# A third input piece queued at once instead of after the second, and 32 more dummy matmuls at the start, in a hybrid decoder block

## The reference

```python
u = rms_norm(h, norm_mix)
q, k, v, z, g_att, g_pool = split(u @ w_in)       # q, k, v: 3 groups x 8 heads x 64
q, k = partial_rope(q, pos), partial_rope(k, pos) # first 16 of 64 dims
att = dilated_attention(q, k, v)                  # (window, dilation): (128,1), (512,4), (2048,16)
pooled = (multiscale_pool(z) @ w_pool_group) * pool_scale
merged = sigmoid(g_att) * (att @ w_att_branch) + sigmoid(g_pool) * (pooled @ w_pool_branch)
h = h + merged @ w_out
f = rms_norm(h, norm_ffn)
h = h + (silu(f @ w_gate) * (f @ w_up)) @ w_down  # D_FF = 2816
return rms_norm(h, norm_final)
```

## Time and profile before

| | |
|---|---|
| median of 3 runs | 1144.56 us (1142.74 to 1144.61) |
| profiled execution | 1144.56 us; its slowest core is core 1 (odd) with a span of 1143.0 us |
| spans of the odd cores 1, 3, 5, 7 | 1143.0, 1134.1, 1136.5, 1134.3 us |
| spans of the even cores 0, 2, 4, 6 | 1128.6, 1130.4, 1128.0, 1132.3 us |
| TensorE busy on core 1 | 1112.9 us, 97% of the span |
| VectorE, ScalarE busy on core 1 | 532.0 us (47%), 448.9 us (39%) |

### The profile page before, as it was taken

How to read it: one execution, slowest core, us unless ns; L and a number is a source line. 1 busy time by engine, 2 the same in 40 slices (tenths; PEclk the granted TensorE clock), 3 DMA queues, 4 the chain that set the end, 5 groups by cost and what they waited for, 6 DMA issues and landing times.

```text
span 1143.0 us, 21157 instructions; the slowest of 8 cores (1128.0 to 1143.0 us)
## 1 busy us (share of the span) xinstructions
PE 1112.9 (97%) x8267; PEld 650.0 (57%) x8267; DVE 532.0 (47%) x795; ACT 448.9 (39%) x725; POOL 69.5 (6%) x135
## 2 busy tenths in 40 slices
PE   5999998999999999999999999999999999999996
PEld 4767766657685867544444444444444444444476
DVE  2478454754763736856543484121223342333244
ACT  2585464675675655562222132111121133231121
POOL 3111000000000000001200000000000000000000
PEclk9899999999999999999999999999999999999999
DMA  8967235227224334152480416443345344641512
GB/s 189 322 178 190 59 79 117 49 62 144 42 58 80 72 80 128 31 142 36 67 198 1 83 30 132 81 74 74 74 75 93 59 88 104 141 91 66 102 72 72
DMA packets 39959, 109.49 MB, mean 96 GB/s; under 512 B 4720, under 2 KB 10992, under 8 KB 36016
## 3 DMA queue, kind: packets, MB, share of 16 engines
q0 software_dynamic: 18800, 68.43, 31.5%
q1 hardware_dynamic: 19760, 38.14, 11.2%
q10 hardware_dynamic: 1296, 1.51, 0.5%
HBM read 145.80 MB, written 15.73 MB: 141 GB/s over the span
## 4 chain that ended last, share of the span: by engine, by line
PE 91%; DMA 4%; DVE 3%; ACT 1%; issue 1%; SPq 0%; DVEq 0%; ACTq 0%
PE ps_all L458 90%; DMA arena<-xs 2%; DVE arena L476 1%; DVE arena L481 1%; ACT arena L466 1%; DMA arena<-sb_1 1%; DMA sa_1<-arena 0%; DMA sb_1<-arena 0%; SPq L323 0%; DVE arena L485 0%; PE ps_all L695 0%; SPq L355 0%; DVE arena L517 0%; DVEq L341 0%; DVEq L348 0%
## 5 line engine op out<-in xcount | busy, mean ns | idle before, releaser
L458 PE MATMUL ps_all<-arena 128*128 128x128 bf16 (+5 forms) x8220 | 1111.6, 299 | 22.3 <-ACT arena L466 9.7
L458 PEld LDWEIGHTS ps_all<-arena 128*128 128x128 bf16 (+1 forms) x8220 | 646.8, 104 | 484.5 <-issue 34.4
L466 ACT ACTIVATE arena<-ps_all 128x512 bf16<-128x512 f32 (+10 forms) x505 | 310.9, 642 | 484.3 <-PE ps_all L458 477.5
L476 DVE TENSOR_TENSOR arena<-arena 128x1024 bf16<-128x1024 bf16 (+14 forms) x314 | 230.7, 754 | 149.0 <-ACT arena L466 117.4
L476 DVE TENSOR_TENSOR arena<-ps_all,arena 128x496 bf16<-128x496 f32 (+4 forms) x160 | 115.3, 730 | 300.7 <-PE ps_all L458 294.1
L466 ACT ACTIVATE arena<-arena 128x512 f32<-128x512 f32 (+8 forms) x187 | 114.9, 632 | 134.6 <-DVE arena L476 99.7
L481 DVE SCALAR_TENSOR_TENSOR arena<-arena 128x512 bf16<-128x512 f32 (+6 forms) x172 | 99.5, 632 | 50.7 <-ACT arena L466 49.5
L481 DVE SCALAR_TENSOR_TENSOR arena<-arena,ps_all 128x496 f32<-128x496 f32 (+1 forms) x64 | 42.0, 665 | 63.5 <-PE ps_all L458 63.2
L323 POOL DMA_DIRECT2D arena<-wq x36 | 19.2, 541 | 247.4 <-PE ps_all L458 245.1
L466 ACT ACT_TABLE_LOAD x13 | 16.7, 1283 | 43.2 <-PE ps_all L458 39.3
L323 POOL DMA_DIRECT2D arena<-wgu x22 | 11.6, 529 | 300.6 <-PE ps_all L458 242.5
(11 more groups left out here) (10 smaller groups left out, 10.8 us busy)
## 6 DMA issues: line engine op xcount, KB each, us to landing
arena<-wgu POOLq DMA_DIRECT2D x22, 1024.0 KB, 8.8
arena<-xT POOLq DMA_DIRECT2D x24, 512.0 KB, 16.2
arena<-wd POOLq DMA_DIRECT2D x8, 1408.0 KB, 10.4
arena<-wq POOLq DMA_DIRECT2D x36, 256.0 KB, 5.6
arena<-wb POOLq DMA_DIRECT2D x24, 256.0 KB, 5.5
arena<-xT SPq DMA_DIRECT2D x8, 768.0 KB, 10.2
oT<-arena SPq DMA_DIRECT2D x24, 248.0 KB, 2.1
arena<-xs POOLq DMA_DIRECT2D x4, 512.0 KB, 24.5
```

Source lines behind the costliest of these rows:

```text
L458: return P.op("pe", lambda e: e.matmul(out, lhsT=lhsT, rhs=rhs, start=start, stop=stop, **kw), [lhsT, rhs], [out], (busy, 0.17))
L466: return P.op("act", lambda e: e.activation(out=out, in_=in_, func=func, **kw), rd, [out], (width(in_) / 1200 + 0.11 + load, 0.08))
L476: return P.op("dve", lambda e: e.tensor_tensor(out=out, in0=in0, in1=in1, op=op), [in0, in1], [out], cost_dve(out, in0, in1))
```

## The change

Two edits. `WARM` of Second goes from 76 to 108. And SyncE no longer waits for the second piece before it issues the third; the line that told the planner that SyncE is busy until 6.0 goes with it. `load_piece` returns nothing any more, which has no effect.

```diff
-WARM = (64, 76)
+WARM = (64, 108)
...
         for lo in range(8 * a, 8 * b, 1024):
-            tok = P.dma(q, f32(K.XS[k][0] + lo, 1024), T["xs"][k][:, lo:lo + 1024])
-        return tok
+            P.dma(q, f32(K.XS[k][0] + lo, 1024), T["xs"][k][:, lo:lo + 1024])
...
     P.dma("sp", cstv, T["cst"])
     load_piece(0, 0, "act")
-    P.wait("sp", [load_piece(0, 1, "sp")])
-    P.free["sp"] = 6.0
+    load_piece(0, 1, "sp")
     load_piece(0, 2, "sp")
```

## The result

The changed kernel takes 1131.8 us (median of 4 runs, 1131.2 to 1132.5; the kernel before beside it 1144.18, 1142.74 to 1144.61). The ratio is 0.9894, 95% interval 0.9877 to 0.9911. The profiled execution took 1132.5 us.

The account below looks back on a forecast made before the run. TensorE, busy for 97% of the slowest core's span, was taken as the bound, so core 1's start counts. 1143.0 - 4.8 - 1.05 = 1137.15 us of span, with 1.56 around it: 1138.7 us; range 1133 to 1146.

Parts of the forecast that it names:

- this wait stays and moves along: At the first scores, near 118 us: TensorE's 2.37 us wait for VectorE's copy remains and shifts earlier; cost 0.
- two terms at the start: Core 1's start: third piece's first query earlier, -4.8 us; less time at the lower clock, -1.05 us.
- The third piece: At the start: lands at 20.5 instead of 25.29, its first query moves from 29.40 to 24.6; -4.8 us.
- The second piece: On SyncE's queue at the start: keeps its landing at 12.43 despite the third piece queued behind it.
- rival 1: At the start: second piece shares the queue with the third and lands near 20.5; +4, 1148.6 us; 14%.
- The weights: On q0 at the start: first key's weights land at 19 or so, key waits about 2 us, covered.
- The clock at the start: On core 1: of 2.8 us lost to half speed, 1.75 stays as on core 0; -1.05 us.
- The two stretches at half speed ... I leave where they are: Near 120 and 185 us on core 1: clock falls stay, 1.7 us lost each; cost 0, -3.4 if they vanish.
- Rival 4: Full speed throughout, start and late stretches: terms -4.8, -2.8 and -3.4, giving 1133.6 us; 10%.
- The dummies: 32 more at Second's start: up to 0.7 us late on core 1, hidden by later waits; taken as 0.

Follow-up runs that it names:

- the transfer alone: Kernel before with only SyncE's wait ahead of the third piece removed, planner's account, order and 76 dummies kept: 1133.81 us, ratio 0.9944.
- the order alone: Changed kernel's order and 108 dummies, but SyncE still waits before issuing the third piece, as in the kernel before: 1138.48 us, ratio 0.9981.

## Why the prediction was wrong

The direction held, and so did the chain at the start; the sum, 5.85 us, was less than half of the 13.7 that core 1 gained. The step that failed is "this wait stays and moves along" at the first scores: a term put at 0 that measured 1.44. With it two terms at the start were too small, by 1.3 and 0.95 us, and 4.5 us came to core 1 behind the first scores, most of it by luck.

- *The third piece* landed at 19.6, not 20.5, and its first query came 3.7 us later, not 4.1: -6.1 for -4.8. The estimate had given it the mean pace of 17 to 25 from 12 on; q1 moved as soon as the second piece was through, 0.5 us sooner than before, and at 0.14 MB per us, the pace of 21 to 25, so the bound at 19.4 was nearer.
- *The second piece* was not slowed (11.9), so rival 1 had no ground.
- *The weights* paid as worked out: the first key's landed at 18.96 (19 expected), and the key waited 1.54 (about 2 expected), hidden as said. That takes the new order: with the old one the late key costs about 1.2 us (the transfer alone, above). Here the rule of the Trainium skill, DMA: Bandwidth & Descriptors, "Issuing engines are not separate DMA queues", agrees with the trace: q0 fell from 0.76 to 0.41 MB between 12 and 17.
- *The clock at the start* was the first wrong choice: core 0's fall was taken as the nearest row, and half of the loss as staying. On all four odd cores it was gone in each profiled execution of the changed kernel, worth 2.0 us on core 1. Core 0 runs another program, and its clock fell only after a second wait of 1.81 that the prediction left out of its reading; for that second wait it had itself worked out 0.6 on core 1. The rule that was set aside for it (the Trainium skill, TensorE: Matmul & The Clock Gate, Part 1: throttled is the default, activity releases it) speaks for the full 2.8; the trace agrees that no fall was left, and not with its size.
- *"This wait stays and moves along"* was the step that failed outright. The order's rows were read as an exchange of a rotation and a norm that adds nothing ahead of the copy. That is so, but that chain begins with a norm that waits for TensorE's statistics, and those of chunk 6 had moved one unit ahead, inside a run of equal matmuls that the printed order merges. With the order alone the wait falls to 0.94, so it is the order's; that it is this one unit is read from the two traces and the two programs and was not tried by itself.
- *"The two stretches at half speed ... I leave where they are"*: both were gone on core 1, for -3.4, but that is mostly luck. The one near 120 came behind the 2.37 us, as on 5 of 12 odd cores with that wait and on none of 40 without, so it goes with the longer wait; yet taking it away on the kernel before left the time as it was. The one near 185 came behind group 2's waits, on which the prediction had no term. On core 1 they were 1.1 us shorter after; over the four odd cores they are the same (2.3 us in the mean before, 2.2 after), and the fall behind them came on two of the four after, core 3 among them, which is now the slowest. Rival 4 had just these terms, at 10%, and was refused since "the later ones" come "after waits that stay"; for group 2's waits that was right.
- *The dummies* at 0 were right for the 32 on the odd cores. That they cost the even cores 2 to 4 us was not foreseen, and does not show in the time, since the odd cores set it.

A part of the miss is which core sets the time. Before, core 1 was 6.5 us behind the next odd core; its first piece landed at 11.07, that of core 3 at 6.69. After, they landed at 10.61 and 10.84, and core 3 gained only 3.2 us in spite of the same mechanism. In the experiments the kernel before took 3 to 4 us less than beside the result and the changed one about the same, and the gain was 8.0 and 9.3 us, which is near the 9.5 that core 1 had gained at the first scores.

## What to carry to other kernels

Where TensorE is the bound, a start that moves earlier can be worth more than its own microseconds if idle times go with it, since in this kernel the granted clock fell behind some of them: count for each later wait whether it lasts, and what clock follows it. Read the same stretch on every core that runs the program before a fall is put into the sum: one core's trace showed two late falls here that the three others didn't have. An estimate that a planner is given moves work far from the edit, so each wait that is said to stay needs the order behind it read unit by unit, merged rows too. And once a gain is in, look for the wait that now ends last: a queue's order (return before fetch) gave another 2.5 to 2.7 us for one condition.

## What the runs showed of the hardware

A third transfer queued behind a second on the same queue left the second's landing as it was (12.43 and 11.9 us), while it nearly halved what another queue moved at that time (0.76 and 0.41 MB in 5 us). Idle times of 2.0 to 2.4 us ahead of the first scores were followed by a fall of the granted clock on 5 of 12 odd cores, those of 0.93 to 0.96 on none of 40. A lower clock at the start need not show in the time: without the uncounted dummies it fell on every odd core and cost 0.2 to 2.0 us up to the first scores, and the changed kernel's time stayed within 1 us, since other cores' late falls set it; with those gone, the same dummies were worth 2.3 us. And with 32 more dummies in one program TensorE stopped for 2.00 us in the opening dummies of the other, on cores that never run them; why is open.
